# First attention's bias rows written 128 times to DRAM and read diagonally, in place of a mirrored read and a matmul with a mirror matrix

## The reference, cut to what matters

```python
def rel_bias_block(rel_bias_g, dilation, n_steps):
    qi = jnp.arange(ATTN_BLOCK)[:, None]
    kj = jnp.arange(2 * ATTN_BLOCK)[None, :]
    steps = jnp.clip(qi + ATTN_BLOCK - kj, 0, n_steps)
    bucket = t5_causal_bucket(steps * dilation)
    return jnp.transpose(rel_bias_g[bucket], (2, 0, 1)).astype(jnp.float32)
...
    logits = jnp.einsum('znqhd,znkhd->znhqk', qb, kw).astype(jnp.float32) * (HEAD_DIM ** -0.5) + bias
    logits = jnp.where(valid[None, :, None], logits, -jnp.inf)
```

## Time and profile before

| what | value |
|---|---|
| median of 3 runs | 2589.32 us (2585.39 to 2589.62) |
| the profiled execution's own time | 2593.13 us |
| its span | 2591.3 us |
| PE busy | 2494.1 us, 96% of the span |
| VectorE (DVE) busy | 1335.6 us, 52% |
| ScalarE (ACT) busy | 1035.0 us, 40% |
| mean granted TensorE clock | 0.985 |
| DMA, mean | 144 GB/s, 44.4% of the 16 DMA engines' time on SP's queue |

### The profile page before, as it was taken

One profiled execution on the slowest core, in us unless ns is written; L12 is line 12 of the kernel. 1 busy time (PEld: TensorE's weight loads), 2 busy tenths in 40 slices (PEclk: granted clock), 3 DMA queues, 4 the chain that ended last, 5 costly groups with the idle time before them and its releaser, 6 DMA issues. The chain is left out here.

```text
span 2591.3 us, 37219 instructions
## 1 busy us (share of the span) xinstructions
PE 2494.1 (96%) x15710; PEld 2161.8 (83%) x15710; DVE 1335.6 (52%) x2198; ACT 1035.0 (40%) x1660; POOL 0.2 (0%) x4
## 2 busy tenths in 40 slices
PE   7999999989999999999888999999999998988999
PEld 6998789978998888888567888888888887878999
DVE  6657454655554333456886433335333337846553
ACT  5534444444433223146562322213222226744443
POOL 0000000000000000000000000000000000000000
PEclk9999999999999999999998999999999999999999
DMA  8986733488862333335102333333333336502564
GB/s 307 306 266 215 244 122 99 139 311 303 313 227 87 94 96 97 98 114 187 58 1 66 90 98 98 98 98 90 98 98 97 95 93 171 186 18 66 175 183 147
DMA packets 146727, 372.28 MB, mean 144 GB/s; under 512 B 20330, under 2 KB 67074, under 8 KB 146562
## 3 DMA queue, kind: packets, MB, share of 16 engines
q1 hardware_dynamic: 146274, 369.59, 44.4%
q10 hardware_dynamic: 288, 0.31, 0.1%
HBM read 368.71 MB, written 1.15 MB: 143 GB/s over the span
## 5 line engine op out<-in xcount | busy, mean ns | idle before, releaser
L298 DVE TENSOR_TENSOR weights_lo<-weights_raw,weights_hi 128x1024 fp32r<-128x1024 f32 (+2 forms) x547 | 657.4, 1212 | 485.0 <-ACT weights_hi L292 482.9
L350 PE MATMUL psum<-normed_hi,weights_hi 128*128 128x256 f32 (+2 forms) x2664 | 884.1, 332 | 22.6 <-DVE normed_lo L629 6.5
L350 PE MATMUL psum<-normed_lo,weights_hi 128*128 128x256 f32 (+2 forms) x2664 | 869.9, 327 | 0.0
L350 PE MATMUL psum<-normed_hi,weights_lo 128*128 128x256 f32 (+2 forms) x2664 | 869.3, 326 | 0.0
L292 ACT CAST weights_hi<-weights_raw 128x1024 fp32r<-128x1024 f32 (+2 forms) x547 | 562.7, 1035 | 374.1 <-DMA weights_raw<-in_w_down 254.3
L350 PEld LDWEIGHTS psum<-normed_hi,weights_hi 128*128 128x128 f32 (+1 forms) x2664 | 512.0, 192 | 86.0 <-issue 35.1
L350 PEld LDWEIGHTS psum<-normed_lo,weights_hi 128*128 128x128 f32 (+1 forms) x2664 | 513.2, 193 | 41.5 <-issue 1.2
L350 PEld LDWEIGHTS psum<-normed_hi,weights_lo 128*128 128x128 f32 (+1 forms) x2664 | 512.9, 193 | 40.7
L350 PE MATMUL psum<-hidden_hi,weights_hi 128*128 128x512 f32 (+1 forms) x594 | 217.6, 366 | 0.0
L350 PE MATMUL psum<-hidden_hi,weights_lo 128*128 128x512 f32 (+1 forms) x594 | 217.1, 365 | 0.0
L350 PE MATMUL psum<-hidden_lo,weights_hi 128*128 128x512 f32 (+1 forms) x594 | 217.0, 365 | 0.0
(11 more groups left out here) (264 smaller groups left out, 2724.1 us busy)
## 6 DMA issues: line engine op xcount, KB each, us to landing
weights_raw<-in_w_gu SPq DMA_DIRECT2D x220, 512.0 KB, 3.6
weights_raw<-in_w_down SPq DMA_DIRECT2D x110, 512.0 KB, 3.6
arena<-in_w_mod SPq DMA_DIRECT2D x72, 512.0 KB, 7.1
weights_raw<-in_w_x SPq DMA_DIRECT2D x24, 512.0 KB, 7.4
resid<-in_w_mod SPq DMA_DIRECT2D x24, 512.0 KB, 7.6
normed_raw<-in_w_mod SPq DMA_DIRECT2D x24, 512.0 KB, 6.9
under_normed_hi<-in_w_mod SPq DMA_DIRECT2D x24, 512.0 KB, 7.2
weights_raw<-in_w_qk SPq DMA_DIRECT2D x24, 512.0 KB, 3.7
```

The costliest lines, as they stand in the source:

```text
L298: ve.tensor_tensor(w_lo[:, c % RING, a], w_raw[:, c % RING, a], w_hi[:, c % RING, a].bitcast(F32), ALU.subtract).then_inc(lo_ready, 1)
L350: last = te.matmul(out, a, b, start=start and n == 0, stop=stop and n == 2)
```

## The change

The 24 rows are written to DRAM 128 times each, so that `scratch_rel` is 24 x 128 x 383 values (4.7 MB in place of 37 KB). The new stage `RelWrites` does it in six transfers of four heads each, issued by SP. The source of a transfer is four partitions, each read 128 times; the destination is 512 rows of 1532 bytes (784,384 bytes in all). The stage is a fourth track of the first segment, from 0.42 to 0.82, with a semaphore of its own (`rel_written`). `RelLoad` waits for it on SP and reads copy p of a head from offset 127 - p in partition p, so the tiles stand the right way round. `rel_rows` moves from the arena to `rstd`, whose next writer (`Gating`, on VectorE) gets a wait for `rel_written`. `RelMirror`, its matrix, its matmuls and its copies go; VectorE waits for the landed tiles (`rel_in`) in the first step of `Attention1`. The attention track now has 20 steps from 0.05 to 0.97.

```diff
-        scratch_rel = nc.dram_tensor("scratch_rel", (NG * HG, TOEP), F32, kind="Internal").ap()
+        scratch_rel = nc.dram_tensor("scratch_rel", (NG * HG, P, TOEP), F32, kind="Internal").ap()
...
-        rel_rows = at(18432, TOEP)
+        rel_rows = rstd[:, 0:TOEP]
...
         class RelRows(Stage):
             def sync(self, sp, i):
                 sp.wait_ge(bias_rows, 2)
                 sp.dma_start(rpb_rows[0:8 * RPB_R, 48:48 + RPB_C], W["rpb"]).then_inc(bias_in, 16)
-                sp.dma_start(scratch_rel, rel_rows[0:NG * HG, :]).then_inc(bias_in, 16)
-                sp.wait_ge(bias_in, 32)
+                sp.wait_ge(bias_in, 16)
                 sp.dma_start(scratch_rpb, rpb_rows[0:8 * RPB_R, :]).then_inc(bias_in, 16)
...
+        class RelWrites(Stage):
+
+            n = NG * HG // 4
+
+            def sync(self, sp, i):
+                heads = slice(4 * i, 4 * i + 4)
+                if i == 0:
+                    sp.wait_ge(bias_rows, 2)
+                again = rel_rows[heads, :].rearrange("p (o n) -> p o n", o=1).to_broadcast([4, P, TOEP])
+                sp.dma_start(scratch_rel[heads], again).then_inc(rel_written, 16)
...
                 if i == SG:
+                    dve.wait_ge(rel_written, 16 * RelWrites.n)
                     for half in range(2):
...
             def sync(self, sp, i):
                 sp.wait_ge(scan_out, SH // 2)
+                sp.wait_ge(rel_written, 16 * RelWrites.n)
                 for s in range(2):
-                    sp.dma_start(relbias[:, :, s, :], bass.AP(scratch_rel.tensor, P * s,
-                                                              [[1, P], [TOEP, NG * HG], [1, P]])).then_inc(rel_in, 16)
-        class RelMirror(Stage):
...
+                    sp.dma_start(relbias[:, :, s, :], bass.AP(scratch_rel.tensor, P * s + P - 1,
+                                                              [[TOEP - 1, P], [P * TOEP, NG * HG], [1, P]])
+                                 ).then_inc(rel_in, 16)
...
                 if u == 0:
-                    pe.wait_ge(rel_ready, 12)
+                    pe.wait_ge(gate_ms, 2)
...
                     dve.wait_ge(a1_scores, i + 1)
+                    if i == 0:
+                        dve.wait_ge(rel_in, 64)
...
             ([RelRows(), DtChain(dt_proj), StateProducts(), TurnX(), Scan(), RelLoad(), Gating(z_proj)], 0.38, 1),
+            ([RelWrites()], 0.42, 0.82),
...
-            ([RelMirror(), Attention1(), TurnAttention1()], 0, 1),
+            ([Attention1(), TurnAttention1()], 0.05, 0.97),
```

More of the change, by code:

```diff
@@ L121, in shape_constants @@
         "ident": np.eye(P, dtype=np.float32),
-        "mirror": np.eye(P, dtype=np.float32)[::-1],
         "mirror64": np.kron(np.eye(2, dtype=np.float32), np.eye(GRID_W, dtype=np.float32)[::-1]),
@@ L258, in build @@
         te, ve, se, ge = nc.tensor, nc.vector, nc.scalar, nc.gpsimd
-        counts = {"bias": 48, "normed": 0, "sums": 0, "norm_sum": 0,
+        counts = {"bias": 32, "normed": 0, "sums": 0, "norm_sum": 0,
                   "norm_av": 0, "norm_vv": 0, "hidden": 0, "heads": 0, "turns": 0, "turned_hi": 0, "pairs": 0, "joint": 0,
@@ L863, in vector @@
                         ve.tensor_scalar(a, a, 0.5, None, ALU.mult)
-        rel_mm = sem("rel_rows_ready")
+        rel_mm, rel_written = sem("rel_rows_ready"), sem("rel_rows_written")
         class RelRows(Stage):
@@ L1065, in vector @@
                 if i == 0:
-                    dve.wait_ge(bias_in, 48)
+                    dve.wait_ge(bias_in, 32)
                 each = dt[:, t * SH + 8 * q:t * SH + 8 * q + 8].rearrange("p (h o) -> p h o", o=1)
@@ L1221, in sync @@
                 sp.wait_ge(scan_out, SH // 2)
+                sp.wait_ge(rel_written, 16 * RelWrites.n)
                 for s in range(2):
-                    sp.dma_start(relbias[:, :, s, :], bass.AP(scratch_rel.tensor, P * s,
-                                                              [[1, P], [TOEP, NG * HG], [1, P]])).then_inc(rel_in, 16)
-        rel_turned, rel_ready = sem("rel_bias_mirrored"), sem("rel_bias_ready")
-        class RelMirror(Stage):
[L1229 to L1247, removed]
+                    sp.dma_start(relbias[:, :, s, :], bass.AP(scratch_rel.tensor, P * s + P - 1,
+                                                              [[TOEP - 1, P], [P * TOEP, NG * HG], [1, P]])
+                                 ).then_inc(rel_in, 16)
         a1_scores, a1_max, a1_exp, a1_turned, a1_copied, a1_pv, a1_out, a1_rows, a1_hi, a1_ready = (
@@ L1621, in __init__ @@
                 self.stat = small[:, 128:128 + 16].rearrange("p (b n) -> p b n", b=4)
-                self.joint0 = take("joint", 0)
                 joint, single = take("joint", 0), take("single", 0)
```

## The result

| | before | after |
|---|---|---|
| median of 4 runs each | 2588.71 us (2585.39 to 2589.62) | 2710.85 us (2705.02 to 2715.85) |
| the profiled execution | 2593.13 us | 2715.85 us |
| its span | 2591.3 us | 2714.1 us |
| mean granted clock | 0.985 | 0.962 |

The changed kernel takes 1.0464 times as long (95% interval 1.045 to 1.0479); the two medians are 122 us apart. The forecast was 2720 us.

What follows compares the result with a forecast made beforehand. PE, busy 96%, was taken to lead, with loads following by 14 us. Mirror -8.5, stalls +131 and clock +8 gave +130.5 us on 2593.1, less 3.8 to the median: 2720 us, range 2580 to 2750.

Steps and rivals of the forecast that it cites:

- What bounds the kernel: PE, busy 96% of the span, leads and loads follow; from 138 to 270 us the DMA engines have least room.
- The six writes, the term that decides: Writes from 138 us: each holds four DMA engines 29.8 us, the high end, and later loads queue behind it.
- the reading of 35 against 27 ns: Packets from crowded neighbouring partitions took 35 ns, those from all 128 partitions 27; thin evidence leaning to slow writes.
- The stalls: From 138 to 270 us: 145.3 us too much DMA work, less 14 of lead, +131 us of PE waits.
- the lead of 14 us: Time by which the DMA engines may fall behind in the weight loads before PE stops: 14 us.
- The clock: After each of six PE stalls the granted clock drops to 1.2 GHz and comes back: +8 us in all.
- The mirror: Six pairs of matmuls leave PE, 10.2 us; the first pair gives nothing, which leaves -8.5 us.
- The costs set at nothing: Wider-spaced attention steps, the waits in `Gating` and `RelLoad`, and the bias read after `rel_in` moves to DVE: zero each.
- Full rate: Rival on the six writes: four engines at full rate, 8.2 us a write, 2587 us; chance 0.28.
- Half way: Rival on the six writes: the shared way carries about two engines' worth, 15 us a write, 2630 us; chance 0.1.
- Hidden: Rival on the six writes: engines held 2 to 6 us a write, nothing stalls, 2581 us; chance 0.12.
- What would show it: Signs: PE waits of 15 to 30 us between 155 and 275 us, DMA share near 0.25 at some 26 GB/s.

Runs made afterwards that it cites:

- x3: The changed kernel with each write of four heads cut into four writes of one head, source one partition read 128 times: 2689.53 us (one run).
- the eight-apart run: The changed kernel with the four source rows of each write eight partitions apart in place of neighbouring: 2588.89 us, 0.9987 of before.
- the kernel with one copy: The changed kernel with each bias row written once in place of 128 times, the biases coming out upside down: 2580.42 us, 0.9957 of before.
- The 32-apart write: A write of the changed kernel with its four source rows 32 partitions apart in place of neighbouring: 2614.89 us (one run).

## Why the prediction was right, point by point

The forecast was 9 us too high, and its path is the one that the runs show: four engines held some 30 us by each write, because of the source. Two terms of its sum were off and partly cancel: the stalls 17 us too long, the clock 6 us too cheap. The range on record, 2580 to 2750 us, took in every rival too, so that the time lies in it says little; the forecast's own range, 2685 to 2755 us, says more.

**What bounds the kernel:** right that PE leads and the loads follow by their lead. But the stretch from 138 us was not short of room for 4.7 MB as such: with 16 sources eight apart it took them at a DMA share of 0.97 and without a gap. What had no room was four engines held 30 us at a time. (Over the first 324 us the DMA slices of before's page read 0.8, 0.9, 0.8, 0.6 and 0.7, not 0.8 to 0.9 throughout.)

**The six writes, the term that decides:** 29.8 us a write on four engines; 31 us by the rate of its packets, 30 to 33 from first to last packet. The bound from the source (four partitions delivered no faster than one engine draws) gave the right size by luck, because two figures happen to be near each other: one engine draws up to 26.3 GB/s, and the shared way brings 25 (steady, after) to 30 (`x3`). What decided between the ends was the reading of 35 against 27 ns, and it pointed the right way: in the eight-apart run the same engines take 67 ns a packet. An issue of a write takes SP 0.7 us, not 0.3 to 0.4, which costs nothing either.

The Trainium skill's rule (SBUF — State Buffer, section "Door 1: The DMA port swizzle") that partitions 0 to 3 lie on one port, at 27.6 GB/s, is borne out as a mechanism, its figure within a tenth. The 28.4 us a write that follow from it lie a little below the measured 30 to 33. That the time which they gave, 2712 us, is so near to 2710.85 us is luck: the write was too short there, the stalls too long for another reason, which follows.

**The stalls:** 131 us predicted, 114.1 us found. This is the term with the largest error. The sum took the stretch from 138 to 270 us as one account, all old load behind the writes and the lead of 14 us once. It is an account for each write: the one write of all rows, alone, holds its engines 31 us and stops PE for 19.0 us, so 12 us are covered, and after's six writes cost 19.0 us each on average. The likely reason, which no run tests by itself, is that the stretch grew with the stalls, to 400 us: a write is issued some 40 us after the last, not 22, and in the 10 to 19 us between the packets of two writes the loads that had to wait come in, at 224 to 299 GB/s, and the lead is had anew. After, from the end of the first write:

```profile
172.00:184.00 12.00, 8.12 (x71) 7.03 (x72) 6.52 (x7) 5.62 (x9) 0.00 (x0) 0.70 0.68 231
```

Why the second stall has 27.3 us and the fifth 14.5 us was not tested. The place that the prediction named for the waits, 155 to 275 us, could not have held 131 us of them; they lie between 159 and 396 us.

**The clock:** 8 us predicted, 14.4 us found. Behind each stall PE's first work runs at the lower level. The windows from the end of the second and of the third stall to the return of the full clock, and the sum over all six such windows:

```profile
226.56:230.40 3.84, 3.84 (x17) 3.62 (x17) 2.29 (x5) 1.52 (x2) 0.00 (x0) 0.50 0.25 44
261.17:268.00 6.83, 6.55 (x37) 4.86 (x38) 3.37 (x6) 2.16 (x3) 0.00 (x0) 0.50 1.00 358
...
sum 29.44, PE 28.85 PEld 23.83 DVE 16.86 ACT 11.32 POOL 0.00; mean PE 4.81 PEld 3.97 DVE 2.81 ACT 1.89 POOL 0.00
```

Half of 28.85 us is lost, 1.7 to 3.3 us a stall and 2.4 on average, where the short wait of before lost 1.4. The account of the first segment closes with it to 0.5 us: of its shift of 129.6 us, 1.6 are there before the first write (the `w_z` load at 136.70 us in place of 135.06), 114.1 are stalls and 14.4 clock.

**The mirror:** -8.5 us predicted, -8.1 measured between the loads in the kernel with one copy, and the wait for L480 went to 4.5 us as foretold. In after the same stretch is 10.9 us shorter than before. The 2.8 us between the two are not the mirror's. From `w_ssm_branch` to `w_out` both kernels take 125.48 us (before 133.96); they differ by 1.3 us ahead of it, where the granted clock is 0.95 in after and 0.90 with one copy, and by 1.5 us behind it, where it is 1.00 and 0.89. DVE's time fell by 7.3 us and gave nothing, as said.

**The costs set at nothing:** the first scores brought no wait, the bias read took 12.2 us in place of 12.9, and the waits in `Gating` and `RelLoad` show no stall of their own, though the sixth write's packets end at 392 us. The writes ended that late, but everything behind them was as late.

**The rivals:** each exists as a kernel now. Full rate: 2588.89 us with four engines on four ports and 9 us a write, where 2587 was worked out, with one wait of 4.6 us, where 5 were. Half way: 2614.89 us at 15 us a write, where 2630 was; again the sum had the stalls too long, 42.5 us against 25. Hidden: 2581.18 and 2581.

**What would show it:** the DMA share of 0.25 with 26 GB/s is there in 2 us windows, and not over a whole stall (0.42 and 0.54 in the windows that begin at 190 and 150 us). The likely reason, not tested, is that the other twelve engines go on with their shares of the chunks behind, up to six slots ahead, and only then stand still.

## What to carry to other kernels

A broadcast write costs by its sources: count how many ways out of SBUF the source partitions span, before the bytes and the engines, and put rows that are read many times on different ones. Eight partitions apart did it here, for four rows and for sixteen; 32 apart did not, since two of the four shared a way, so a larger distance is not a safer one. Or build the rows on more partitions. A transfer that holds a few DMA engines holds every later transfer of its queue, since each needs a share on all; so the price of a slow transfer is set by what is queued behind it and by the lead of those loads (31 us held, 12 covered, 19 lost), and it is paid again for each such transfer once the lead has come back. And where a wait is put down to an odd step of a merged order, follow the releaser's own idle time back until it ends at a transfer.

## What the runs showed that was not expected

- **A write begins at full speed.** DMA of after, the first microsecond of the first write, 141.9 to 142.9 us:

```profile
DMA packets 85, 0.17 MB, mean 166 GB/s; under 512 B 10, under 2 KB 65, under 8 KB 85
```

  Of the 65 packets under 2 KB ten are under 512 bytes, so 55 are the write's, in 1 us; later it is 36 in 2.2 us, in the window from 145.1 us. The first microsecond alone would have given the price of full rate; whether a small write would as well was not tried. The 32-apart write has 62 packets in the 1 us from 141 us and 32 in that from 147 us, the all-in-one write 272 in the 2 us from 142 us and 188 in those from 146 us, so there the start lasts some 3 us.

- **One partition read by 16 engines gives 27 to 30 GB/s, four neighbours read by four engines 25.** More readers on one way bring little.

- **The clock stays at the lower level through the idle time.** In the stall from 242 to 261 us PE did nothing, and the granted clock was first partly and then wholly at the lower level (1.2 GHz):

```profile
245.00:250.00 5.00, 0.00 (x0) 0.00 (x0) 0.00 (x0) 0.00 (x0) 0.00 (x0) 0.75 0.51 103
250.00:256.00 6.00, 0.00 (x0) 0.00 (x0) 0.00 (x0) 0.00 (x0) 0.00 (x0) 0.50 0.45 97
```

  So most of the time at 0.50 lies over idle time, and only the work just behind the stall is slowed, up to the return of the full clock. Ten times the idle time costs less than twice the clock: 1.9 us behind 27.3 us of idle, 1.4 us behind 2.8. The length of the stall doesn't order it either: the most, 3.3 us, is lost behind the one of 18.8 us.
